# A two-layer model kernel: the first layer's modulation in two parts, and three large products of the delta-rule layer as float32r sums

## The reference

```python
m = jax.nn.silu(cvec) @ w + b                 # adaln_params: 1024 x 6144 weights, split in 6 parts
h  = modulate(x,  norm1_g[i], sh1, sc1)       # rmsnorm(x, g) * (1 + scale) + shift
p = h @ w_in                                  # gdn_project: 1024 x (4*1024 + 32)
qkv = jax.nn.silu(centred_depthwise_conv(p[..., :3 * GDN_WIDTH], conv_w))
z = p[..., 3 * GDN_WIDTH:4 * GDN_WIDTH]
q = l2norm(heads(qkv[..., :GDN_WIDTH])) * GDN_DK ** -0.5
k = l2norm(heads(qkv[..., GDN_WIDTH:2 * GDN_WIDTH]))
...
o = rmsnorm(o, norm_g) * jax.nn.silu(z.reshape(b, l, h, dv))
return o.reshape(b, l, h * dv) @ w_out        # gdn_out
...
x = x + g1 * y
x = x + g2 * peer_ffn(modulate(x, norm2_g[i], sh2, sc2), ...)
```

## Time and profile before

| | us |
|---|---|
| median of 3 runs | 4753.47 |
| lowest, highest | 4753.03, 4755.95 |
| the profiled execution | 4752.16 |
| its span in the trace | 4750.4 |

### The profile page before, as it was taken

How to read it: one execution, slowest core, us unless ns; L and a number is a source line. 1 busy time by engine, 2 the same in 40 slices (tenths; PEclk the granted TensorE clock), 3 DMA queues, 4 the chain that set the end, 5 groups by cost and what they waited for, 6 DMA issues and landing times. The chain is left out here.

```text
span 4750.4 us, 59992 instructions
## 1 busy us (share of the span) xinstructions
PE 3886.5 (82%) x20597; PEld 2722.1 (57%) x20597; DVE 2271.8 (48%) x4462; ACT 1534.1 (32%) x2599; POOL 170.7 (4%) x148
## 2 busy tenths in 40 slices
PE   5987998986859999999878559999628776777766
PEld 2437997443748877777655559998426422222222
DVE  0435664169956666666535968888352200000001
ACT  1223333021844444444324157666112211111111
POOL 0003342000000000000000000000000000000000
PEclk7978999998979999999989789999757888878888
DMA  7100001043474444444321159996321199999996
GB/s 282 68 3 1 1 1 57 15 176 117 141 225 172 175 174 175 175 173 174 139 74 45 36 179 366 317 318 234 129 90 69 46 428 427 428 427 428 428 428 279
DMA packets 302741, 904.93 MB, mean 190 GB/s; under 512 B 18672, under 2 KB 138736, under 8 KB 277104
## 3 DMA queue, kind: packets, MB, share of 16 engines
q1 hardware_dynamic: 302576, 902.68, 50.2%
HBM read 851.24 MB, written 51.38 MB: 190 GB/s over the span
## 5 line engine op out<-in xcount | busy, mean ns | idle before, releaser
L1678 PE MATMUL pd<-h_parts,u_parts 128*128 128x512 f32 x2048 | 484.8, 395 | 47.0 <-DVE u_parts L1764 47.0
L1691 PE MATMUL po<-act_parts,v_parts 128*128 128x512 f32 x2048 | 481.6, 392 | 11.0 <-DVE v_parts L1769 8.3
L1678 PEld LDWEIGHTS pd<-h_parts,u_parts 128*128 128x128 f32 x2048 | 384.4, 188 | 141.8 <-DVE u_parts L1764 47.2
L2801 PE MATMUL pb<-moe_ring,moe_xs 128*32 128x512 f32 x2048 | 333.2, 762 | 136.8 <-DMA moe_ring<-in_moe_gu 124.1
L1691 PEld LDWEIGHTS po<-act_parts,v_parts 128*128 128x128 f32 x2048 | 382.6, 188 | 105.4 <-DVE v_parts L1769 23.0
L2852 DVE TENSOR_TENSOR moe_hidden<-moe_silu,pg 128x512 f32<-128x512 f32 x16 | 11.0, 687 | 657.8 <-PE pg L2790 531.6
L1884 PE MATMUL pd<-h_parts,u_parts 128*128 128x256 f32 x2048 | 265.6, 283 | 43.4 <-DVE u_parts L1963 43.4
L1884 PEld LDWEIGHTS pd<-h_parts,u_parts 128*128 128x128 f32 x2048 | 262.2, 191 | 53.6 <-DVE u_parts L1963 43.9
L296 PE MATMUL ps<-hT,w_stream 128*128 128x512 f32 (+1 forms) x672 | 269.4, 564 | 27.8 <-ACTq L316 27.8
L1894 PE MATMUL po<-v_parts,act_parts 128*128 128x512 f32 x1024 | 255.4, 392 | 0.2 <-DVE act_parts L1979 0.2
L2817 PE MATMUL pd<-moe_ring,moe_hidden 128*32 128x512 f32 x1024 | 161.0, 763 | 108.8 <-DMA moe_ring<-in_moe_down 95.3
(11 more groups left out here) (449 smaller groups left out, 6285.1 us busy)
## 6 DMA issues: line engine op xcount, KB each, us to landing
moe_ring<-in_moe_gu SPq DMA_DIRECT2D x128, 2048.0 KB, 26.8
u_stream<-in_peer_u SPq DMA_DIRECT2D x256, 512.0 KB, 6.3
v_stream<-in_peer_v SPq DMA_DIRECT2D x256, 512.0 KB, 5.1
moe_ring<-in_moe_down SPq DMA_DIRECT2D x64, 2048.0 KB, 26.0
ada_ring<-in_ada_w SPq DMA_DIRECT2D x24, 2048.0 KB, 18.1
peer_gates<-gate_stage SPq DMA_DIRECT2D x6, 8192.0 KB, 30.3
g_stream<-peer_gates SPq DMA_DIRECT2D x128, 256.0 KB, 5.0
w_stream<-in_gdn_w_in SPq DMA_DIRECT2D x8, 2048.0 KB, 8.2
```

Of the source, the lines that this page charges most:

```text
L1678: m = pe.matmul(pd[:, j, 0:T], us[:, j, w, c], h[:, w, c], start=(c + w == 0), stop=(c == DC - 1 and w == 1))
L1691: m = pe.matmul(po[:, (c + b) % 4, 0:T], vs[:, j, w, (c + b) * P:(c + b) * P + P], aparts[:, 4 * half + j, w], start=(j + w == 0), stop=(j ...
L2801: m = pe.matmul(pb[32 * q:32 * q + 32, n % 2, :], xs[:, u % 2, c], w[:, c, :], start=(c < 4), stop=(c >= 4))
```

## The change

The modulation is made in two parts. The first stage makes 4 of the 12 groups (parts 0 and 1). The other 8 are a second `AdaParams` object: its vector of conditions is made behind `gdn_qkv`, its first four fetches are issued as `linear_tok` begins, and its products stand inside the first `normalise_heads`, one group behind every second head that is spread; `finish` follows.

The three large products (q/k/v, z, output) go through a new `linear_split`. Each operand is the sum of a float32r value and a float32r remainder, and three of the four products of these terms are added (the product of the two remainders is left out). `split_terms` makes the terms of the activations in a block of its own ahead of each product. The terms of the weights are made chunk by chunk, two chunks ahead, by ScalarE (`high_w`) and VectorE (`low_w`), in a ring of three. The buffer `raw` shrinks from 24 chunks to 2. In `normalise_heads` the row of roots is split in two terms too, and each head is spread by two float32r multiplications in place of one of float32.

```diff
--- before.py
+++ after.py
...
@@ -341,7 +341,107 @@
     psum_free.done(BANKS + chunks)
 
 
-def linear_tok(k, hT, kc, tiles, out, stream):
+def split_terms(k, src, kc, parts):
+    high = k.sig("tt_high")
+    with k.nc.Block() as block:
+        @block.scalar
+        def _(act):
+            for c in range(kc):
+                act.activation(parts[:, 0, c], src[:, c], ACT.Copy).then_inc(high.h, 1)
+        @block.vector
+        def _(dve):
+            for c in range(kc):
+                dve.wait_ge(high.h, high.at(c + 1))
+                dve.tensor_tensor(parts[:, 1, c], src[:, c], parts[:, 0, c].bitcast(F32), ALU.subtract)
+    high.done(kc)
+def linear_split(k, parts, kc, T, n, evac, stream, engine="scalar", after=None, beside=None):
+    nc = k.nc
+    made, psum_free = k.sig("lin_made"), k.sig("lin_psum_free")
+    high, split = k.sig("px_u_high"), k.sig("px_u_split")
+    groups, chunks = n // BANK, n // P
+    per = BANK // P
+    BANKS, RING, AHEAD = 4, 3, 2
+    wb, loaded = stream.wb, stream.loaded
+    with ExitStack() as ctx:
+        ws = k.sb(ctx, "w_terms", [RING, 2, kc, P], F32R)
+        ps = k.banks(ctx, BANKS)
+        def raw(ch):
+            return wb[:, ch // per % 2, :, ch % per * P:ch % per * P + P]
+        with nc.Block() as block:
+            @block.sync
+            def _(sp):
+                for g in range(2, groups):
+                    sp.wait_ge(split.h, split.at((g - 1) * per))
+                    stream.fetch(sp, g, g % 2)
+            @block.tensor
+            def _(pe):
+                for ch in range(chunks):
+                    pe.wait_ge(split.h, split.at(ch + 1))
+                    pe.wait_ge(psum_free.h, psum_free.at(ch + 1))
+                    r = ch % RING
+                    for c in range(kc):
+                        for w, x in ((0, 0), (0, 1), (1, 0)):
+                            m = pe.matmul(ps[:, ch % BANKS, 0:T], ws[:, r, w, c], parts[:, x, c], start=(c + w + x == 0), stop=(c == kc - 1 and w == 1))
+                    m.then_inc(made.h, 1)
+            def high_w(act, ch):
+                if ch < chunks:
+                    act.wait_ge(loaded[ch // per % 2].h, loaded[ch // per % 2].at(DMA_DONE * (ch // (2 * per) + 1)))
+                    if ch >= RING:
+                        act.wait_ge(made.h, made.at(ch - RING + 1))
+                    act.activation(ws[:, ch % RING, 0], raw(ch), ACT.Copy).then_inc(high.h, 1)
+            def low_w(dve, ch):
+                if ch < chunks:
+                    dve.wait_ge(high.h, high.at(ch + 1))
+                    dve.tensor_tensor(ws[:, ch % RING, 1], raw(ch), ws[:, ch % RING, 0].bitcast(F32), ALU.subtract).then_inc(split.h, 1)
+            def empty(eng, ch):
+                eng.wait_ge(made.h, made.at(ch + 1))
+                evac(eng, ps[:, ch % BANKS, 0:T], ch).then_inc(psum_free.h, 1)
+                if after:
+                    after(eng, ch)
+            @block.scalar
+            def _(act):
+                if engine == "scalar":
+                    act.sem_inc(psum_free.h, BANKS)
+                for ch in range(AHEAD):
+                    high_w(act, ch)
+                for ch in range(chunks):
+                    high_w(act, ch + AHEAD)
+                    if engine == "scalar":
+                        empty(act, ch)
+            @block.vector
+            def _(dve):
+                if engine == "vector":
+                    dve.sem_inc(psum_free.h, BANKS)
+                for ch in range(AHEAD):
+                    low_w(dve, ch)
+                for ch in range(chunks):
+                    low_w(dve, ch + AHEAD)
+                    if engine == "vector":
+                        empty(dve, ch)
+                    elif beside:
+                        beside(dve, ch, psum_free, psum_free.at(BANKS + 1) + ch)
+    loaded[0].done(DMA_DONE * -(-groups // 2))
+    loaded[1].done(DMA_DONE * (groups // 2))
+    for x in (made, high, split):
+        x.done(chunks)
+    psum_free.done(BANKS + chunks)
+def linear_tok(k, hT, kc, tiles, out, stream, begin=()):
...
+            if begin:
+                @block.sync
+                def _(sp):
+                    for x in begin:
+                        x.begin(sp)
+
...
+
+    def __init__(self, k, ctx, layer, ada_w, params, consts, mod, fetch=True, first=0, groups=6 * D // BANK):
         nc = k.nc
         self.layer, self.params, self.mod = layer, params, mod
+        self.first, self.GROUPS = first, groups
         self.stacked = CONSTS(consts, "stacked")
...
+        at = (self.first + g) * BANK
+        sp.dma_start(self.ring[:, g % self.TURN], self.src[:, :, at:at + BANK]).then_inc(self.slot[g % self.TURN].h, DMA_DONE)
+
+    def begin(self, sp):
+        for g in range(self.TURN):
+            self.fetch(sp, g)
...
-        ada = AdaParams(k, ctx, layer, ada_w, params, consts, mod)
+        ada = AdaParams(k, ctx, layer, ada_w, params, consts, mod, groups=4)
...
-        linear_T(k, hT, DC, TALL, 3 * D, evac, stream=stream, after=squash, beside=convolve)
+        linear_split(k, parts, DC, TALL, 3 * D, evac, stream=stream, after=squash, beside=convolve)
...
+        terms = k.sb(ctx, "nh_terms", [2, T], F32R)
+        pick = k.sb(ctx, "nh_pick", [16], F32R)
...
+            if ada:
+                @block.sync
+                def _(sp):
+                    ada.sync(sp)
...
+                act.activation(pick[rows], CONSTS(consts, "ident")[rows, 0:16], ACT.Copy)
+                act.wait_ge(chain.h, chain.at(2))
+                act.activation(terms[rows, 0], r[rows], ACT.Copy).then_inc(root.h, 1)
+                if ada:
+                    for g in range(ada.GROUPS):
+                        ada.scalar(act, g)
...
-                pe.wait_ge(chain.h, chain.at(2))
+                pe.wait_ge(root.h, root.at(2))
+                pe.wait_ge(chain.h, chain.at(3))
                 for h in range(heads):
                     if h >= 4:
                         pe.wait_ge(used.h, used.at(h - 3))
-                    sel = CONSTS(consts, "ident")[rows, h:h + 1].broadcast_to([16, P])
-                    pe.matmul(pw[:, h % 4, 0:T], sel, r[rows], start=True, stop=True).then_inc(spread.h, 1)
+                    sel = pick[rows, h:h + 1].broadcast_to([16, P])
+                    pe.matmul(pw[:, h % 4, 0:T], sel, terms[rows, 0], start=True, stop=False)
+                    pe.matmul(pw[:, h % 4, 0:T], sel, terms[rows, 1], start=False, stop=True).then_inc(spread.h, 1)
+                    if ada and h % 2:
+                        g = h // 2
+                        ada.tensor(pe, g)
+                        if g:
+                            ada.turn(pe, g - 1)
+                if ada:
+                    ada.turn(pe, ada.GROUPS - 1)
 
             @block.vector
             def _(dve):
...
+                dve.wait_ge(root.h, root.at(2))
+                link(dve.tensor_tensor(terms[rows, 1], r[rows], terms[rows, 0].bitcast(F32), ALU.subtract))
...
             with ExitStack() as c2:
                 w_ab = Stream(k, c2, W["gdn_w_in"][:, 4 * D:4 * D + 32], DC, bufs=1)
-                w_qkv = Stream(k, c2, W["gdn_w_in"][:, 0:3 * D], DC)
-                modulated(k, 0, xT, TALL, hT, C("one"), params, mod, "norm1_g", 0, begin=(w_qkv, w_ab))
-                raw = k.sb(c2, "qkv_raw", [24, 2, SEQ + 4])
-                gdn_qkv(k, hT, params, qkvT, raw, w_qkv)
-                linear_tok(k, hT, DC, 4, ab, w_ab)
+                with ExitStack() as c3:
+                    w_qkv = Stream(k, c3, W["gdn_w_in"][:, 0:3 * D], DC)
+                    modulated(k, 0, xT, TALL, hT, C("one"), params, mod, "norm1_g", 0, begin=(w_qkv, w_ab))
+                    raw = k.sb(c3, "qkv_raw", [2, 2, SEQ + 4])
+                    parts = k.sb(c3, "h_terms", [2, DC, TALL], F32R)
+                    split_terms(k, hT, DC, parts)
+                    gdn_qkv(k, parts, params, qkvT, raw, w_qkv)
+                ada = AdaParams(k, c2, 0, W["ada_w0"], params, consts, mod, fetch=False, first=4, groups=8)
+                linear_tok(k, hT, DC, 4, ab, w_ab, (ada,))
+                normalise_heads(k, qkvT[:, 0:16], 16, TALL, consts, 1.0, lambda h: float(P) ** -0.5 if h < 8 else 1.0, ada=ada)
+                ada.finish(k)
             qT, kT, vT = qkvT[:, 0:8, :], qkvT[:, 8:16, :], qkvT[:, 16:24, :]
-            normalise_heads(k, qkvT[:, 0:16], 16, TALL, consts, 1.0, lambda h: float(P) ** -0.5 if h < 8 else 1.0)
             k_tok = k.sb(ctx, "k_tok", [4, 8, P])
             v_tok = vT.rearrange("p (t a) (b n) -> p t a b n", t=4, n=P)
...
+            parts = k.sb(ctx, "h_terms", [2, DC, TALL], F32R)
             normalise_heads(k, oT, 8, TALL, consts, 1.0 / P, lambda h: PARAMS(params, "gdn_norm_g"), (w_z, w_out))
+            split_terms(k, hT, DC, parts)
...
-                dve.tensor_tensor(o, o, zT[:, bass.ds(ch, 1), :], ALU.mult)
-            linear_T(k, hT, DC, TALL, D, evac_z, stream=w_z, beside=times_z)
```

(40 more changed lines are left out.)

1 line of the change is left out of this document (removed).

## The result

| | before | after |
|---|---|---|
| median of 4 runs, us | 4754.5 | 4698.11 |
| lowest, highest | 4753.03, 4755.95 | 4697.26, 4698.38 |
| span in the trace | 4750.4 | 4696.2 |

The changed kernel takes 0.9881 of the time before (95% interval 0.9864 to 0.9898): 56.4 us less, where 30 less were forecast. The kernel before was measured again beside the experiments, at 4750.42 and 4752.35; each of them is held against the one measured with it.

The account below looks back on a forecast made before the run. Fetches were taken to bound the first modulation, TensorE the q/k/v, z and output products. Terms, chiefly -46.0 (modulation), +12.3 (q/k/v) and +7.6 (first normalisation), sum to -30.0: 4722.2, stated as 4723; range 4706 to 4747.

Parts of the forecast that it names:

- q/k/v cycle: Q/k/v product: Silu, `high_w`, `low_w`, convolution wait in turn, 7.2 us a cycle, TensorE needing 5.64; +12.3 us for the stage.
- The prediction's own test: Q/k/v product: copies out 7.2 us apart expected; 6.9 or less would refute the chain, 8 or more the clock.
- the first modulation: First stage with four groups, bound by fetches: `mod` written at about 41.9 in place of 87.93, -46.0 us.
- the second object: Second modulation object: a memset and a Silu in blocks of their own, +1.1 us; its four fetches covered.
- the second normalisation: 16 float32r multiplications at 0.427 take 6.8 us in place of 13.71, the root row costs 1.5: -5.3 us.
- the entry of a split product: Ahead of q/k/v, z and output: activation terms, a block boundary and first weights, 8.3 us each with TensorE standing.
- the spreading: First normalisation with eight groups: 36 us, nearer the fetches, before 28.4; +7.6 us, ends +5 and +28.4.
- z and output: The z and output products: 56.5 us each against 58.03 and 56.87, so -1.5 and -0.4 us.
- Given back: Rival, first normalisation: the clock stays low, it ends after 56.8 us, +28.4, 4744 in all; chance 0.20.
- The clock falls in q/k/v: Rival, q/k/v product: TensorE's pauses lower its clock, 10.25 us a chunk, +75 on the forecast, 4798; chance 0.05.
- The chain is no bound: Rival, q/k/v product: weight split overlaps the convolution, 5.64 us a chunk holds, -34, 4689; chance 0.04.
- The change does less: Rival, whole change: straight-coded products and splits cost more than their rows and the groups come late, 4738 to 4752; chance 0.09.

Follow-up runs that it names:

- e1_straight: The kernel before with the loops of the q/k/v product written out, still float32, nothing else changed; 4749.13 us against 4750.42, ratio 0.9998.
- e4_order: The changed kernel with the q/k/v weight split moved: `high_w` between copy out and Silu, `low_w` behind the convolution; 4680.05 us, ratio 0.9855 to the kernel before.
- e2_mod_only: The kernel before with the two-part modulation alone, products and spreading still in float32; 4734.08 us, ratio 0.9968 to the kernel before.
- e2b_mod_only_again: The same kernel as `e2_mod_only` (kernel before with the two-part modulation alone) in another profile; 4734.31 us.
- e6_both: The changed kernel with the edits of `e4_order` and `e5_merge` joined; 4665.76 us, ratio 0.9816 to the kernel before.
- e3_linears_only: The changed kernel with all 12 modulation groups back in the first stage, split products and root terms kept; 4719.4 us, ratio 0.9937 to the kernel before.
- e5_merge: The changed kernel with the activations' terms made inside each product's block, behind the first chunk's weights; 4682.47 us, ratio 0.9856 to the kernel before.
- e7_terms_apart: The changed kernel with the three term products reordered so no weights are used twice in a row; 4697.61 us, ratio 0.9887 to the kernel before.

## Why the prediction was off by 25 us

**The step that failed** is in the q/k/v cycle: "4.34 (convolution to Silu, 198.30 to 202.64)". The mechanism was right; the term was measured in looped code and used for written-out code. It is 3.66 in the changed kernel and 3.67 in `e1_straight`, 0.68 less. The rest of the 0.79 by which the cycle missed is in the hand-overs: `low_w` starts 1.08 us behind `high_w`, and the convolution starts 1.14 behind `low_w`, where 1.11 and 1.22 were taken. Over 21 cycles that is some 16.5 us. The first Silu came 12.2 us behind the first multiplication in place of 14.6: the table load (1.3), for which the prediction had an allowance, hid, and the convolution was 0.7 shorter here too. The entry added 7.8 us, not 8.3. The two last cycles took 4.82, not 5.80: the same 0.67, and 0.31 between the copy out and the convolution (0.92 in the earlier trace rows, 0.61 after). In sum the stage missed by 21 us.

The prediction's own test misled too: copies 6.9 us apart or less "would refute the chain". They were 6.42 apart and the chain was the bound, as `e4_order` shows. What marks a chain is the releaser of the idle time; the period alone does not.

**Right in mechanism and size:** the first modulation; the second object; the root row; the second normalisation, where a 16-row float32r multiplication at the lower clock starts every 0.43 us, the taken end of 0.427 to 0.47; the entry of a split product, which added 7.8, 8.0 and 8.0 us where 8.3 was taken. That the first modulation agrees to 0.4 us is partly luck: in the seven traces with four groups `mod` is written between 40.62 and 43.01.

**Right in size, not in its bound:** the spreading took 34.9 us where 36 were worked out. The forecast put it down to the fetches, with waits for `ada_ring`. There is one such wait, of 0.44 us, and TensorE is busy in 34.36 of the 34.90: the first pair of heads with its group ran at the lower clock (5.5 us, 275.60 to 281.14), the others followed 3.95 apart. The clock did rise during the group products, as the forecast had it.

**z and output** missed by 2.0 and 2.8 us. Of each, 1.5 is the price of a record (192 times 0.008) and 0.3 the entry. Output also lost less to its start at the lower clock: 45.69 less 0.4 is 1.8 us above eight chunks of 5.44, where 2.7 was taken. (The prediction's 3.1 and 1.7 for the slow starts before are not alike: the 0.3 of latency is taken off the second alone; with it off the first too, that is 2.8.) The Trainium skill (FP8 and Floating Point Precision, TensorE Precision Notes) gives float32 four passes through the array. With one pass for each product of terms, three of the four would be 5.15 us a chunk, an estimate. The trace has 5.44, which is 79% of the 6.87 before.

**The rivals.** *Given back:* not in this kernel (clock 0.91), but true of the modulation alone (0.67). *The clock falls in q/k/v:* no. In the window 118 to 232 of the kernel after the granted clock is 0.99, with a pause of TensorE in every cycle. The Trainium skill (TensorE: Matmul & The Clock Gate, A second HAM failure mode) tells of a kernel in which frequent small idles between groups of multiplications made the clock swing. Here 0.67 us in every 6.42 did not. *The chain is no bound:* its time, 4689, is nearer to the measured 4698 than the forecast, but the mechanism is refuted by `e4_order`. *The change does less:* no.

**The later stages** lost 4.4 us that no step foresaw; with the 1.0 gained in untouched stages before them that is 3.4, above the 3 that the prediction named as the mark of being wrong altogether. Most of it is 3.2 us in two untouched products of the memory layer. They are 15.49 and 14.05 us long before, 16.95 and 15.74 after. But two executions of one kernel, `e2_mod_only` and `e2b_mod_only_again`, differ in just this way. Timeline of the first, then of the second:

```profile
3627.98 15.46 PE L296 MATMUL ps<-mem_hT,w_stream 128*128 128x256 f32 x64 [6.54 <-ACTq L316]
3645.77 14.05 PE L296 MATMUL ps<-memT,w_stream 128*128 128x256 f32 x64 [2.33 <-ACTq L316]
```

```profile
3625.71 17.09 PE L296 MATMUL ps<-mem_hT,w_stream 128*128 128x256 f32 x64 [6.63 <-ACTq L316]
3645.12 15.74 PE L296 MATMUL ps<-memT,w_stream 128*128 128x256 f32 x64 [2.33 <-ACTq L316]
```

The granted clock over the two products is 0.91 and 1.00 in the first, 0.82 and 0.89 in the second. So these 3 us come and go with the execution and need no change of the code. Nor do they show in the whole: the second execution is 3.3 us shorter in the stages between the output product and the memory layer, and its span is only 1.1 us longer. Of the other profiles, `e1_straight` and `e6_both` have the short form, `e3_linears_only`, `e4_order`, `e5_merge` and `e7_terms_apart` the long one. What decides it is open, and so is whether the change makes the long form more frequent.

## What to carry to other kernels

A duration read from a trace belongs to its form of code as well as to its operation: before using it for code that is written out, look whether the row's neighbours have small waits of a constant size between them (0.18 us here, gone in the written-out code). When a product gets cheaper on TensorE, write down the order of the helpers on the other engines first: here exchanging two instructions on ScalarE and making the inputs inside the product's block gave 32 us, beside the 56 of the whole change. And a group in the timeline can hold a pause; take the price of one from a group that is not fed by another engine.

## What the runs showed of the hardware

- The five dependent VectorE operations of the convolution, up to the Silu behind them: 4.34 us in a loop (kernel before), 3.67 written out (`e1_straight`).
- ScalarE's table load (1.28 us) starts beside the convolution in written-out code (124.69 in `e1_straight`, 87.38 in the changed kernel), ahead of what its activation waits for, and hides there. In the loop of the kernel before it starts behind the convolution (135.19) and the Silu behind it (136.49).
- One float32r multiplication with 512 columns starts every 0.227 us at the full clock (128 rows, chunks of 24 in 5.44 us) and every 0.427 at the lower one (16 rows, second normalisation); loading the same weights twice in a row makes no difference (46.47 us for 192 in both orders, `e7_terms_apart`).
- A busy TensorE can stay at its lower clock: 0.50 over 14.1 us of 16-row float32r multiplications without a pause (`e3_linears_only`). Eight group products with 16-row float32 multiplications between them got 0.67, with float32r ones 0.91.
- Single executions of one kernel differ by 3 us in a stage, with the granted clock in it (0.91 and 1.00 against 0.82 and 0.89 over two products).
